# Three attention layers in 32-bit on one core: roots spread and state-space products issued in the middle of a projection tile

## What is computed

```
def rms_norm(x, w):
    y = x32 * lax.rsqrt(jnp.mean(x32 * x32, axis=-1, keepdims=True) + EPS)
...
# differential attention (layer 1)
q = rms_norm(q, diff_q_norm_w[j])
k = rms_norm(k, diff_k_norm_w[j])
o = rms_norm(diff_attention(q, k, v, lam), diff_subln_w[j]) * (1.0 - lambda_init)
...
# state-space mixer (layer 2)
decay = jnp.exp(jnp.where(tri, seg, -jnp.inf))
cb = jnp.einsum('bclgn,bcsgn->bcgls', cm, bm)
scores = cb[:, :, :, None] * decay
y_diag = jnp.einsum('bcgels,bcsgep->bclgep', scores, xdt)
...
y = y_diag + y_off + d_skip.astype(jnp.float32).reshape(SSD_GROUPS, e)[:, :, None] * x6
...
# forgetting attention (layer 2)
qh = rms_norm_2(heads(q), q_norm_w)
kh = rms_norm_2(heads(k), k_norm_w)
```

## Time and profile before

| | |
|---|---|
| median of 3 runs | 1104.93 us |
| lowest, highest | 1104.47, 1109.87 us |
| profiled execution, its own time | 1107.31 us |
| its span | 1105.5 us |
| TensorE busy (matmul) | 1061.1 us, 96% of the span |
| VectorE busy | 760.7 us, 69% |
| ScalarE busy | 594.6 us, 54% |
| GpSimd busy | 178.3 us, 16% |
| DMA queue 1, share of 16 engines | 48.0% |
| TensorE's share of the chain that ended last | 81% |

### The profile page before, as it was taken

The page is one execution under the profiler, slowest core; times in us unless marked ns, Lnnn a source line. Parts: engine busy times, 40 slices in busy tenths (PEclk is TensorE's granted clock), DMA queues, the critical chain, the costliest instruction groups (busy, mean ns, idle before and its releaser), DMA issues.

```text
span 1105.5 us, 24083 instructions
## 1 busy us (share of the span) xinstructions
PE 1061.1 (96%) x8706; PEld 1022.2 (92%) x8706; DVE 760.7 (69%) x1331; ACT 594.6 (54%) x1071; POOL 178.3 (16%) x186
## 2 busy tenths in 40 slices
PE   5999999999999998899999999989899999999998
PEld 5989999999999887899999999988788999999998
DVE  6765686666555876876565548858777669988843
ACT  6654564444544744554444446655655556666532
POOL 4000121111110000321111110000111123444300
PEclk9999999999999999999999999989999999999999
DMA  7533455555665322455555664433232355555563
GB/s 281 177 123 107 128 174 189 180 180 183 176 194 169 118 82 54 162 182 182 178 190 164 192 198 150 162 128 116 79 113 87 115 200 174 188 180 181 164 209 104
DMA packets 51480, 174.45 MB, mean 158 GB/s; under 512 B 5840, under 2 KB 7120, under 8 KB 51280
## 3 DMA queue, kind: packets, MB, share of 16 engines
q1 hardware_dynamic: 51408, 173.46, 48.0%
HBM read 172.39 MB, written 1.05 MB: 157 GB/s over the span
## 4 chain that ended last, share of the span: by engine, by line
PE 81%; DVE 12%; ACT 3%; issue 2%; POOL 1%; DMA 0%; SPq 0%; DVEq 0%; POOLq 0%; ACTq 0%
PE bank L650 24%; PE bank L651 24%; PE bank L652 24%; DVE ring_lo L1403 3%; DVE xw_lo L1409 1%; PE bank L744 1%; ACT tmp L1168 1%; PE bank L758 1%; PE bank L855 1%; PE bank L933 1%; PE bank L815 1%; PE bank L835 1%; POOL scratch L1328 1%; DVE x L1481 1%; DVE root_parts L1586 0%
## 5 line engine op out<-in xcount | busy, mean ns | idle before, releaser
L650 PE MATMUL bank<-xw_hi,ring_hi 128*128 128x256 f32 x1736 | 500.2, 288 | 3.2 <-ACT lam L1303 1.1
L651 PE MATMUL bank<-xw_lo,ring_hi 128*128 128x256 f32 x1736 | 492.9, 284 | 0.0
L652 PE MATMUL bank<-xw_hi,ring_lo 128*128 128x256 f32 x1736 | 492.7, 284 | 0.0
L1403 DVE TENSOR_TENSOR ring_lo<-ring_raw,ring_hi 128x1024 fp32r<-128x1024 f32 (+2 forms) x338 | 402.2, 1193 | 57.0 <-ACT ring_hi L987 51.4
L987 ACT ACTIVATE ring_hi<-ring_raw 128x1024 fp32r<-128x1024 f32 (+2 forms) x338 | 341.2, 1012 | 88.9 <-PE bank L652 81.7
L650 PEld LDWEIGHTS bank<-xw_hi,ring_hi 128*128 128x128 f32 x1736 | 334.7, 193 | 11.8 <-issue 6.5
L651 PEld LDWEIGHTS bank<-xw_lo,ring_hi 128*128 128x128 f32 x1736 | 334.8, 193 | 0.2
L652 PEld LDWEIGHTS bank<-xw_hi,ring_lo 128*128 128x128 f32 x1736 | 334.6, 193 | 0.0
L650 PE MATMUL bank<-act_hi,ring_hi 128*128 128x256 f32 x768 | 221.3, 288 | 12.1 <-DVE ring_lo L1788 7.6
L651 PE MATMUL bank<-act_lo,ring_hi 128*128 128x256 f32 x768 | 219.0, 285 | 0.0
L652 PE MATMUL bank<-act_hi,ring_lo 128*128 128x256 f32 x768 | 218.8, 285 | 0.0
(11 more groups left out here) (177 smaller groups left out, 926.8 us busy)
## 6 DMA issues: line engine op xcount, KB each, us to landing
ring_raw<-w_up SPq DMA_DIRECT2D x132, 512.0 KB, 3.2
ring_raw<-w_in SPq DMA_DIRECT2D x85, 512.0 KB, 3.2
ring_raw<-w_down SPq DMA_DIRECT2D x48, 512.0 KB, 3.6
ring_raw<-w_down SPq DMA_DIRECT2D x24, 384.0 KB, 3.8
ring_raw<-w_ob SPq DMA_DIRECT2D x10, 512.0 KB, 3.5
ring_raw<-w_oa SPq DMA_DIRECT2D x16, 256.0 KB, 2.7
ring_raw<-w_oa SPq DMA_DIRECT2D x8, 512.0 KB, 3.7
ring_raw<-w_kv SPq DMA_DIRECT2D x7, 512.0 KB, 6.5
```

The source lines that it names most:

```text
L650: mm(bank[b][:, 0:T], w_hi, tile(hi, t), start=kk == 0, stop=False)
L651: mm(bank[b][:, 0:T], w_hi, tile(lo, t), start=False, stop=False)
L652: last = mm(bank[b][:, 0:T], w_lo, tile(hi, t), start=False, stop=end)
L1403: V.tensor_tensor(ring_lo[:, a:b], ring_raw[:, a:b], ring_hi[:, a:b].bitcast(f32), SUB).then_inc(lo_done, 1)
```

## The change

On TensorE, in layers 1 and 2, `spread` is no longer done behind tile s but in the middle of the next one: `project` calls `halfway(c)` before the block that begins its second half. In layer 2 `ssd_out` is moved in the same way, behind the spread where both are due. Layer 0 and all other steps stay. The weights `ssd_w` get four buffers: heads 0 and 1 of every four lie in `tmp`, heads 2 and 3 in the area of `dist` and `distT`; ScalarE's exponentials wait for the product before the last. As that area is `halo`'s too, its zero columns are set again before the last up projection. On VectorE, in layers 1 and 2, `ssd_skip` and `norm_out` go to the end of a slot's EARLY steps.

```
--- before.py
+++ after.py
@@ -365,8 +365,10 @@
         def ret_bank(h):
             return bank[(7, 3)[h % 2]]
 
+
         def ssd_w(h):
-            return tmp[:, 1920 + (h % 2) * 384:2304 + (h % 2) * 384]
+            room, a = (tmp, 1920) if h % 4 < 2 else (con, CCOL["dist"])
+            return room[:, a + (h % 2) * 384:a + 384 + (h % 2) * 384]
 
         gate_s, gate, val, prod = (tmp[:, a:a + 512] for a in (0, 512, 1024, 1536))
         conv_out, tap_c, tap_a, tap_b = (tmp[:, a:a + 512] for a in (512, 1024, 2048, 2560))
@@ -623,7 +625,7 @@
         def _(pe):
             mm = nc.tensor.matmul
 
-            def project(ph, i, c, hi, lo, ready):
+            def project(ph, i, c, hi, lo, ready, halfway=None):
 
                 slot, g = ph.tile(i, c)
                 n = ph.out(i, c)
@@ -638,6 +640,8 @@
                         pe.wait_ge(out_ready, freed)
                 last = None
                 for k in range(ph.blocks[part]):
+                    if halfway and k == ph.blocks[part] // 2:
+                        halfway(c)
                     kk = part * 8 + k
                     t = ph.inputs[kk]
                     if first and c < ph.per:
@@ -684,10 +688,10 @@
                 pe.wait_ge(ss_done, KT * (q + 1))
                 mm(bank[7][:, 0:T], cmat("ones1024"), sqsum, start=True, stop=True).then_inc(ms_done, 1)
 
-            def run(name, hi, lo, ready, q=None, then=None):
+            def run(name, hi, lo, ready, q=None, then=None, halfway=None):
                 ph = PH[name]
                 for c in range(ph.body):
-                    project(ph, 0, c, hi, lo, ready)
+                    project(ph, 0, c, hi, lo, ready, halfway)
                     if c == (1 if name == "kv" else 0) and q is not None:
                         mean_square(q)
                     if then:
@@ -931,7 +935,7 @@
                 for tt, (q, width) in enumerate(((0, T), (P, P))):
                     for n in range(2):
                         last = mm(bank[5][64 * n:64 * n + 64, q:T], tok(x_tok, (2 * p + n) * 64, 64, tt),
-                                  ssd_w(n)[:, tt * T:tt * T + width], start=tt == 0, stop=tt == 1)
+                                  ssd_w(2 * p + n)[:, tt * T:tt * T + width], start=tt == 0, stop=tt == 1)
                 last.then_inc(ss_y, 1)
 
             DO = {"norm": norm, "spread": spread, "group_norm": group_norm, "turn": turn, "ret_scores": ret_scores, "ret_out": ret_out,
@@ -939,12 +943,23 @@
                   "ssd_decay": ssd_decay, "ssd_out": ssd_out, "fox_scores": fox_scores,
                   "fox_weights": fox_weights, "fox_values": fox_values}
 
+            HALFWAY = ((), ("spread",), ("spread", "ssd_out"))
+
             def follow(layer, slot0):
                 def then(c):
                     for kind, *key in PLAN[layer][slot0 + c]:
-                        if kind in DO:
+                        if kind in DO and kind not in HALFWAY[layer]:
                             DO[kind](layer, *key)
                 return then
+
+            def amid(layer, slot0):
+
+                def halfway(c):
+                    if slot0 + c:
+                        for kind, *key in PLAN[layer][slot0 + c - 1]:
+                            if kind in HALFWAY[layer]:
+                                DO[kind](layer, *key)
+                return halfway
 
             run("kv", act_hi, act_lo, stream_ready(0), 0)
             for layer in range(3):
@@ -955,8 +970,8 @@
                        start=True, stop=True).then_inc(lam_ps, 1)
                     pe.wait_ge(lam_e, 1)
                 n_in = PH[f"in{layer}"].n
-                run(f"in{layer}", xw_hi, xw_lo, stream_ready(q), q, follow(layer, 0))
-                run(f"oa{layer}", act_hi, act_lo, mixed_ready(layer), None, follow(layer, n_in))
+                run(f"in{layer}", xw_hi, xw_lo, stream_ready(q), q, follow(layer, 0), amid(layer, 0))
+                run(f"oa{layer}", act_hi, act_lo, mixed_ready(layer), None, follow(layer, n_in), amid(layer, n_in))
                 project_group(layer)
                 run(f"up{layer}", xw_hi, xw_lo, stream_ready(q + 1), q + 1)
                 run(f"down{layer}", act_hi, act_lo, ffn_ready(layer))
@@ -1209,8 +1224,8 @@
                 act.wait_ge(ss_bc, h + 1)
                 if h == 0:
                     act.wait_ge(act_small, 7)
-                if h >= 2:
-                    act.wait_ge(ss_y, h // 2)
+                if h >= 4:
+                    act.wait_ge(ss_y, h // 2 - 1)
                 for tt, (a, width) in enumerate(((0, T), (T, P))):
                     last = A(ssd_w(h)[:, a:a + width], bank[7][:, a:a + width], ACT.Exp,
                              bias=tok_neg[:, 16 * tt + h:16 * tt + h + 1])
@@ -1764,7 +1779,10 @@
 
             def follow(layer, slot0, kinds):
                 def steps(ph, i, c):
-                    for kind, *key in PLAN[layer][slot0 + c]:
+                    planned = PLAN[layer][slot0 + c]
+                    if layer and kinds is EARLY:
+                        planned = sorted(planned, key=lambda step: step[0] in ("ssd_skip", "norm_out"))
+                    for kind, *key in planned:
                         if kind in kinds:
                             DO[kind](layer, *key)
                 return steps
@@ -1831,6 +1849,8 @@
                 if layer < 2:
                     run(f"up{layer}", swiglu_evac(layer), swiglu_after(layer), q + 1)
                     run(f"down{layer}", add_to_x, into_stream(q + 2), unrolled=True)
+            V.memset(halo.rearrange("p (b c) -> p b c", b=2)[:, :, 0:4], 0.0).then_inc(halo_zero, 1)
+            dve.wait_ge(halo_zero, 2)
             run("up2", halo_evac, None, 6, before_split=conv_before, end=conv_end)
             run("down2", add_to_x, None, unrolled=True)
 
```

1 line of the change is left out of this document (removed).

## The result

| | before | after |
|---|---|---|
| median of 6 runs each | 1108.28 us | 1099.88 us |
| lowest, highest | 1104.47, 1110.42 us | 1098.47, 1103.28 us |
| profiled execution, its own time | 1107.31 us | 1101.83 us |
| its span | 1105.5 us | 1099.9 us |
| DMA queue 1, share of 16 engines | 48.0% | 47.3% |

The ratio is 0.9932, with a 95% interval of 0.9915 to 0.9949: the change saves 0.68%, more than the 0.5% that a measurement can tell. The forecast was 1098.8 us (1093.5 to 1104.0), from a median of 1104.9 for the kernel before; with three more runs that median is 3.4 us higher. As differences: forecast -6.1, medians -8.4, profiled executions -5.5.

A forecast was written before the change was run, and what follows sets the result against it. TensorE was taken as the bound, with 12.6 us of waits for roots and decayed weights as the target. Layer 1 at -1.8 and layer 2 at -4.3 gave -6.1 from 1104.9: 1098.8 us, range 1093.5 to 1104.0.

The forecast's parts named there:

- Rival 3: VectorE becomes the bound, each of 18 readouts delaying evacuation and split: about +10 us, 1115 us; chance 0.07.
- Rival 4: Both mixing layers: waits are only passed on, nothing measurable changes, 1104 to 1106 us; chance 0.08.
- rival 2: VectorE keeps up better, new waits at slot 32 and tile 20 under 1 us: -10.5, 1094.4 us; chance 0.18.
- Rival 1: The clock is not relieved, new waits cost as many half-speed stretches as old: 1101.8 to 1104 us; chance 0.22.
- Slot 25: Layer 1: the 0.91 us wait goes, the 1.04 us wait at the second output stage grows as much: 0.
- The readout soon: Layer 1, slot 18: norm 70's readout ahead of the scores on VectorE: +2.6 us at tile 20, +1.5 half-speed stretch.
- The sorted order: Layer 2, skip and readout behind softmax: slot 32 +2.7 wait, +1.5 half speed; slots 38 and 44 +1.5 us.
- Of the 6.8 us at half speed I keep one half: Layer 2, slots 20 and 21, at product 1: half the half-speed stretch goes, -1.7 us (-3.4 to 0).
- clock terms: Half-speed stretches in layers 1 and 2, each charged to the waits ahead of it: -3.0 of the -6.1 us.
- the stretch at 444.3: Layer 1: this half-speed stretch follows a wait for softmax and stays.
- With four buffers ... that is off the path: Layer 2, slots 20 and 21: head 4's exponentials need not wait for the product; no time credited.
- The cost of broken tiles: Tiles broken open at 26 pieces: taken as 0, bounded by 0.12 us each, 3.1 us in all.

The follow-up runs named there:

- e6: Changed kernel with only the spread of norm 70 (layer 1) back behind its tile: 1096.88 us, ratio 0.9904 to the kernel before.
- e5: Changed kernel with layer 2's VectorE steps in the old order, skip and readout ahead of softmax and weights: 1093.79 us, ratio 0.9874 to the kernel before.
- e2: Changed kernel with mid-tile steps and sorted order in layer 2 only, layer 1 issued as before: 1099.97 us, ratio 0.9928 to the kernel before.
- e4: Changed kernel with only layer 2's products in mid tile, sorted order kept there, layer 1 as before: 1103.86 us, ratio 0.9960 to the kernel before.
- e3: Changed kernel with only layer 2's spreads in mid tile, sorted order kept there, layer 1 as before: 1110.47 us, ratio 1.0026 to the kernel before.
- e7: Changed kernel with two buffers of decayed weights instead of four: 1103.08 us, ratio 0.9963 to the kernel before.
- e11: Changed kernel with old order in layer 2, norm 70's spread back behind its tile, and two weight buffers: 1090.78 us, ratio 0.9836 to the kernel before.
- e9: Changed kernel with layer 0's six spreads in mid tile as well: 1100.26 us, ratio 0.9924 to the kernel before.
- e8: Changed kernel with old order in layer 2 and norm 70's spread back behind its tile: 1091.34 us, ratio 0.9853 to the kernel before.
- e10: e8 with layer 2's gate of pair 0 on VectorE one slot later: 1089.13 us, ratio 0.9821 to the kernel before.

## Why the prediction was right, and where not

**Direction, size and place** held: faster, with the most of it in layer 2. That the time itself came out within 1.1 us is in part luck: the kernel before is 3.4 us slower than the median I started from, and the gain 2.3 us larger than I forecast. In the trace the forecast had layer 1 at -1.8 (measured -2.0) and layer 2 at -4.3 (measured -6.9). Rival 3 (VectorE the bound) is out: there is no wait of TensorE for `ring_lo` in either mixing stage. Rival 4 (nothing measurable) is out, and so is rival 2: the new waits came, at the sizes of the forecast. Rival 1 (the clock is not relieved) is half right: layer 2's half-speed time fell from 10.2 to 3.4 us, layer 1's didn't fall, and layer 0, which nothing touched, had 10.2 instead of 3.4, so that the profiled executions hold 23.8 us of it before and after. The difference of these two executions (-5.5) is smaller than that of the medians, and layer 0's +2.5 is a part of the reason.

**Waits.** Layer 2: those that should go were forecast at -7.0 (1.8, 2.8, 1.3 and 1.1), and they fell from 8.5 to 1.5. The new ones were put at +2.7 and +1.5, and are 2.7 and 1.7. Layer 1: -2.9 net at the roots against -3.7, with one of 0.4 left, over the 0.3 that I had named as the most; the `act_lo` wait of over 2 us in tile 20 is there with 2.46 (the working had over 3). Slot 25 came out as written: the wait at the second output stage is still 1.04 us, now with a further one of 0.59 ahead of it:

```profile
458.81 0.39 PE L677 MATMUL bank<-act_hi,ring_hi 128*128 128x256 f32 x1 [0.59 <-POOL act_lo L1371]
...
460.48 0.39 PE L677 MATMUL bank<-act_hi,ring_hi 128*128 128x256 f32 x1 [1.04 <-POOL act_lo L1371]
```

**The two costs of the change, and their causes, are shown.** "The readout soon" in layer 1 was to cost 2.6 + 1.5 = 4.1; e6, which undoes that spread alone, gives back 3.5 of the stage. The sorted order was to cost 2.7 + 1.5 + 1.5 = 5.7 in layer 2; e5 gives back 5.9. Both are one mechanism: a TensorE step asked for later, or a VectorE step placed later, is paid for by what is queued behind it.

**The step that failed in layer 2 is the clock:** "Of the 6.8 us at half speed I keep one half". All of it went, and half-speed time in that stage fell from 10.2 to 3.4 us where I had it fall by 3.4 (6.8 gone, 3.4 new). The clock terms of my sum there are -1.7 - 1.3 + 1.5 = -1.5, those of the waits -2.8. TensorE's windows of the whole stage in before, after and e2:

```profile
665.01:914.48 249.47, 237.72 (x1948) 0.98 0.39 129
666.34:908.94 242.60, 233.63 (x1949) 0.99 0.39 133
666.85:907.87 241.02, 232.09 (x1948) 1.00 0.40 134
```

The time that isn't busy fell from 11.75 to 8.97 us: -2.8, as forecast. The error of 2.6 is in the busy time, which fell by 4.1 for the same work. After and e2 run the same code there with the same waits and differ by 1.54 us of busy time, for one stretch; at that price two stretches fewer are -3.1, twice what I had. The remaining 1.0 agrees with something that I hadn't priced: a wait costs more than its idle time. Idle time counts from the end of a matmul (0.28), while with no wait the next starts after 0.12; and the first one behind a wait starts 0.22, not 0.12, ahead of the second (435.41 and 435.63 in before). That is about 0.26 us for each wait, an estimate from these rows. The view of waits, 652 to 900 us, has 13 of them before and 9 after. e4 points the same way: with no stretch and 12 waits it was busy 233.06 us, 1.0 more than e2 with 9.

**In layer 1 the sum (-1.8 against -2.0) was right by luck, by parts that were not.** I had two stretches of three gone and one new. But the stage held 10.2 us at half speed before and after: the stretch at 444.3 that should stay is gone, and one of 6.8 us lies at 434.1, one of 3.4 at 461.4. And what the roots gave, 3.7 us, came back as other waits: all rows of TensorE's waits in this stage add to 9.8 us before and after. The same 10.2 us slowed fewer matmuls, though: 24 and 19 against 20, 18 and 18, since TensorE stood idle for 1.2 us of the stretch at 434.1. At 1.1 us for some 18 of them (e3, below), 13 fewer are worth about 0.8, an estimate. About one microsecond of the 2.0 stays open. What e6 gives back is accounted for: its rows add to 7.3, 2.5 less than after, and one stretch less (1.1) makes 3.6 of the 3.5.

**"With four buffers ... that is off the path" was wrong** for the kernel as changed: without them it loses 3.4 us (e7). It holds for the old order (e11). I had costed the edit by itself, and not beside the sorted order, which had used up VectorE's slack in slot 32.

**The cost of broken tiles**, taken as 0 with a bound of 3.1 us for 26 pieces, is 0 as far as e9 can tell for six, and a spread takes 0.69 us in either place.

**The clock terms could not be counted on one by one.** Layer 1's unchanged code took 128.75, 128.72 and 129.07 us (before, e2, e4) with 10.2 us at half speed, and 126.49 in e3 with 3.4, though the waits for the roots in e3 were no shorter: 4.7 us in all, longest 1.8. This agrees with what the Trainium skill, "TensorE: Matmul & The Clock Gate", Part 1, says of the slow matmuls at a kernel's start, whose number differs from run to run for the same kernel; by it the sum would have been -3.1, less than any of the differences measured. So the rule speaks against reading a single stretch as the price of a single wait. Fewer and shorter waits often went with less half-speed time: none is left in layer 2 of e5, e8, e10 and e11. But none was there in e2 and e4 either, with waits of up to 2.7 and 1.9 us, and e2's code is after's, which had one stretch.

## What to carry to other kernels

If a consumer stands still for a short time for a result that comes by itself a little later, asking for it in the middle of the next group of matmuls, with its own bank, is free on TensorE and takes the wait away. But follow the result on: whatever reads it stands in another engine's queue, in order, and if it stands early there it holds back all behind it (3.5 us for one such step here). Put a step that waits for a slow partner behind the cheap ready ones and not ahead, and leave what can run in an engine's idle time in that idle time (5.9 us for sorting it out of there); and when one of two moves is costed, cost it beside the other, since a wait can be the cover for the next one. Where both are tested one at a time, take a third change that goes with them out of both, or its cost is counted twice.

## What had not been expected

- A stretch of 3.4 us at half clock has no single price, and mostly costs less than the 1.5 I took. Layer 0, whose code is the same in all but e9, took 133.56 us with none, 134.06 with one (before), 134.81 and 134.87 with 6.2 to 6.4 us of it, 135.85 to 135.87 with 6.8, 136.39 to 136.60 with 10.2: 0.5 us for the one of before, 1.0 on the average of three. Layer 1's 128.75 and 126.49 differ by two stretches, 1.13 each. In layer 2 the same code differs by 1.6 for one (e2 and after).
- Unchanged layer 0 thereby varied by up to 4.2 us (133.56 to 137.78), more than two thirds as much as the forecast for the whole change. A comparison of two spans would have mixed it with the effect.
- A part of the change was slower than no change: layer 2's spreads with the sorted order, by 0.26% (0.10 to 0.42). The spreads' waits went and the products' grew by as much, so that the cost of the sorted order was left.
